# Router of the experts: low halves of x on another engine, exponentials ahead of a copy, a quarter of a product behind the ranks

## The reference, cut to what matters

```
h = rmsnorm(x, norm_ffn_g)
g_prob = softmax(h @ w_rg + b_rg);  g_top, g_idx = top_k(g_prob, 1)
e_in   = (h @ w_re + b_re)[group g_idx]
e_top, e_idx = top_k(softmax(e_in), 2)
wts = g_top * e_top / sum(e_top)
x = x + sum over the token's two experts e: wts * ((silu(h @ w_g[e]) * (h @ w_u[e])) @ w_d[e])
x = x + (p @ w_ple) * sigmoid(rmsnorm(x, norm_ple_g) @ w_ple_gate)
return rmsnorm(x, final_norm_g)
```

## Time and profile before

| | us |
|---|---|
| median of 3 runs | 1081.22 (1079.3 to 1083.87) |
| profiled execution | 1086.42 |
| its span (first to last instruction) | 1084.6 |
| TensorE busy | 1036.2 |
| VectorE busy | 627.4 |
| ScalarE busy | 534.5 |
| GpSimd busy | 89.8 |

### The profile page before, as it was taken

How to read it: one execution, slowest core, us unless ns; L and a number is a source line. 1 busy time by engine, 2 the same in 40 slices (tenths; PEclk the granted TensorE clock), 3 DMA queues, 4 the chain that set the end, 5 groups by cost and what they waited for, 6 DMA issues and landing times.

```text
span 1084.6 us, 15375 instructions
## 1 busy us (share of the span) xinstructions
PE 1036.2 (96%) x6023; PEld 795.3 (73%) x6023; DVE 627.4 (58%) x1235; ACT 534.5 (49%) x940; POOL 89.8 (8%) x104
## 2 busy tenths in 40 slices
PE   6998999999999999899999999998989999999987
PEld 5776589999988877599999889676754454545445
DVE  4677567888745566568888647757752121212155
ACT  5766465565535465556555435856532221212254
POOL 0101001122100311001212101100000000000000
PEclk8998699999999999999999999999999999999989
DMA  8824135655554533255664564224739999999921
GB/s 280 297 79 154 40 118 178 197 170 192 197 194 155 195 118 120 73 170 180 183 200 162 196 181 135 97 90 142 280 112 410 409 409 408 409 409 409 403 93 39
DMA packets 112672, 224.62 MB, mean 207 GB/s; under 512 B 10559, under 2 KB 65234, under 8 KB 112594
## 3 DMA queue, kind: packets, MB, share of 16 engines
q1 hardware_dynamic: 112434, 223.04, 58.7%
q10 hardware_dynamic: 160, 0.53, 0.1%
HBM read 222.50 MB, written 1.05 MB: 206 GB/s over the span
## 4 chain that ended last, share of the span: by engine, by line
PE 87%; DVE 6%; ACT 4%; issue 1%; DMA 1%; SPq 0%; DVEq 0%; ACTq 0%
PE ps L542 82%; PE ps L546 4%; DVE wl L1862 1%; ACT pb L1332 1%; DMA ring<-in_w_uv_dram 1%; DVE smb L1876 1%; ACT wh L1335 1%; ACT hh L1332 1%; DMA cst<-in_const_dram 0%; DVE hl L1872 0%; ACT L1332 0%; DVE ml L1862 0%; DVE pb L1867 0%; ACT mh L1335 0%; DVE sA L1872 0%
## 5 line engine op out<-in xcount | busy, mean ns | idle before, releaser
L1862 DVE TENSOR_TENSOR wl<-ring,wh 128x1024 fp32r<-128x1024 f32 (+3 forms) x212 | 278.1, 1321 | 128.4 <-ACT wh L1335 127.2
L1335 ACT ACTIVATE wh<-ring 128x1024 fp32r<-128x1024 f32 (+3 forms) x212 | 222.7, 1053 | 145.5 <-PE ps L542 145.0
L542 PE MATMUL ps<-hh,wh 128*128 128x256 f32 x768 | 219.0, 286 | 0.4 <-DVE big L1880 0.3
L542 PE MATMUL ps<-hh,wl 128*128 128x256 f32 x768 | 217.2, 284 | 0.0
L542 PE MATMUL ps<-hl,wh 128*128 128x256 f32 x768 | 215.4, 284 | 0.0
L542 PEld LDWEIGHTS ps<-hh,wh 128*128 128x128 f32 x768 | 147.7, 192 | 1.8 <-issue 1.4
L542 PEld LDWEIGHTS ps<-hh,wl 128*128 128x128 f32 x768 | 147.8, 192 | 0.0
L542 PEld LDWEIGHTS ps<-hl,wh 128*128 128x128 f32 x768 | 146.8, 192 | 0.2
L542 PE MATMUL ps<-ring,xg 128*64 128x512 f32 x320 | 85.5, 595 | 0.0
L542 PE MATMUL ps<-wh,hh 128*128 128x512 f32 (+3 forms) x192 | 80.2, 418 | 4.4 <-DVE wl L1862 4.3
L2702 POOL TENSOR_TENSOR fs<-fs,rt 128x256 f32<-128x256 f32 x44 | 52.4, 1213 | 322.8 <-ACT fs L1332 322.8
(11 more groups left out here) (284 smaller groups left out, 1715.7 us busy)
## 6 DMA issues: line engine op xcount, KB each, us to landing
ring<-in_w_up_dram SPq DMA_DIRECT2D x88, 512.0 KB, 4.7
ring<-in_w_down_dram SPq DMA_DIRECT2D x22, 1024.0 KB, 4.9
ring<-in_w_gate_e_dram SPq DMA_DIRECT2D x40, 512.0 KB, 7.9
ring<-in_w_up_e_dram SPq DMA_DIRECT2D x40, 512.0 KB, 9.3
ringx<-in_w_down_e_dram SPq DMA_DIRECT2D x16, 1024.0 KB, 8.6
ring<-in_w_down_e_dram SPq DMA_DIRECT2D x16, 1024.0 KB, 9.9
ring<-in_w_in_odd_dram SPq DMA_DIRECT2D x12, 1024.0 KB, 5.1
ringx<-in_w_gate_e_dram SPq DMA_DIRECT2D x24, 512.0 KB, 9.9
```

Source lines behind the costliest of these rows:

```text
L542: return e.matmul(o, l, r, start=start, stop=stop)
L1335: return e.activation(o, i, ACT.Copy)
L1862: return e.tensor_tensor(o, a, b, op)
```

## The change

Three edits.

1. The low halves move from VectorE to GpSimd, one behind the other, each behind its high half.
2. On ScalarE the exponentials of the logits come ahead of the high half of tile 1.
3. On TensorE the last quarter of the embeddings' product, (1, 1), comes behind the ranks; with it moves the point at which its weights' slot is free.

```diff
@@ tensor
-            for t in range(2):
-                for n in range(2):
-                    b = claim(2 * t + n, "ple", t, n)
-                    for k in range(2):
-                        w = mm(b[:, :], ppT[:, k, t * P:(t + 1) * P], up[:, k, n * 512:(n + 1) * 512], k == 0, k == 1)
-                    w.then_inc(of(full, "ple", t, n), 1)
-            unit_done[u_ple] = (of(full, "ple", 1, 1), use["ple", 1, 1][1] + 1)
+
+            def embedding(t, n):
+                b = claim(2 * t + n, "ple", t, n)
+                for k in range(2):
+                    w = mm(b[:, :], ppT[:, k, t * P:(t + 1) * P], up[:, k, n * 512:(n + 1) * 512], k == 0, k == 1)
+                w.then_inc(of(full, "ple", t, n), 1)
+
+            for t, n in ((0, 0), (0, 1), (1, 0)):
+                embedding(t, n)
             q.wait_ge(s_msk, 1)
             b = take("rank")
...
+            embedding(1, 1)
+            unit_done[u_ple] = (of(full, "ple", 1, 1), use["ple", 1, 1][1] + 1)
@@ scalar
-            copy(xhk[:, 1], xk[:, 1]).then_inc(s_xhi, 1)
             q.wait_ge(s_smi, 1)
             act(scr[:, 0:80], scr[:, 0:80], ACT.Exp).then_inc(s_sme, 1)
+            copy(xhk[:, 1], xk[:, 1]).then_inc(s_xhi, 1)
@@ vector
-            def x_lo(t):
-                q.wait_ge(s_xhi, t + 1)
-                tt(xlk[:, t], xk[:, t], xhk[:, t].bitcast(F32), ALU.subtract).then_inc(s_xlo, 1)
...
-            x_lo(0)
             b = filled(q, "route")
...
-            x_lo(1)
             b = filled(q, "rank")
@@ gpsimd
+            for t in range(2):
+                q.wait_ge(s_xhi, t + 1)
+                e.tensor_tensor(xlk[:, t], xk[:, t], xhk[:, t].bitcast(F32), ALU.subtract).then_inc(s_xlo, 1)
```

## The result

The changed kernel is slower: 1088.01 us median of 21 runs against 1083.38 of 21 of the kernel before, ratio 1.0044 with a 95% interval of [1.0031, 1.0058], some 4.7 us.

What follows compares the result with a forecast made beforehand. TensorE, busy for 96% of the span, was taken to bound the kernel. Order -1.72, VectorE's loss behind the ranks +0.3 and clock -1.35 sum to -2.8 us: 1078.4 against 1081.22, range 1075.3 to 1083.0.

Steps and rivals of the forecast that it cites:

- The place: Router up to the first expert's product: an earlier first product moves the rest of the kernel one for one.
- The quarter behind the ranks: TensorE ahead of the ranks: ranks start 1.72 us earlier with all edits, only 0.9 us without the other two.
- The clock gain of 1.35 us: Gather on TensorE: no clock fall after the ranks, so 3.85 us instead of 5.19.
- The gain of the logits taken early: VectorE's chain to the mask: logits taken at 782.5 instead of 784.22, 1.7 us earlier.
- Rival D: Experts behind the gather: DMA at 1.03 could hold them back and swallow the gain; 1081 us, chance 0.06.
- What GpSimd costs VectorE: VectorE's small operations beside GpSimd: slowed by 0.7 us up to the mask, 0.3 us lost behind the ranks.
- The upper end that I gave, 5.5 us: VectorE between exponentials and mask: at most 0.25 us lost on each of 22 small operations, ranks at 794.9.
- rival B: VectorE's small operations lose over 0.85 us, 0.1 each putting the mask at 791.6; 1079.8 to 1080.8 us, chance 0.12.
- right behind the third quarter: Ranks on TensorE: forecast to start at 790.24, when three quarters of the embeddings' product are done.
- if it had no cover: Last quarter between ranks and gather: hidden in idle time with 0.2 us to spare, otherwise costing its 1.72 us back.
- GpSimd's own duration: Each low half on GpSimd: 5.3 us taken, from 3.05 x 1.74, between ends of 3.05 and 8.6 us.
- Rival C: Low halves on GpSimd late for the gather, up to 8.6 us each, gather 3.9 us later; 1085.1 us, chance 0.12.

Runs made afterwards that it cites:

- e3: Kernel before with only the last quarter of the embeddings' product moved behind the ranks; ratio 0.9980 to the kernel before.
- e1: Changed kernel with both low halves back on VectorE at their old places, the other two edits kept; ratio 0.9990 to the kernel before.
- e4: Changed kernel with GpSimd computing one feature of 128 per tile, the gather reading high halves in place of low; ratio 0.9965 to the kernel before.
- e5: Changed kernel with each low half cut into eight GpSimd operations of 128 features; ratio 1.0006 to the kernel before.
- e6: Changed kernel with each low half computed twice on GpSimd, the second behind the first; ratio 1.0089 to the kernel before.
- e2: Kernel before with only the low halves moved to GpSimd, old order on ScalarE and TensorE; ratio 1.0039 to the kernel before.

## Why the prediction was wrong

**What held.** The place: experts follow the router one for one (30.73 us for two steps in both), and the stretch's 4.06 us are close to the 4.7 of the medians. The quarter behind the ranks gains by itself: in e3 the ranks start 0.77 us earlier, "only 0.9 us" in the prediction. The clock gain of 1.35 us, where TensorE does not stand idle ahead of the ranks for long: from the gather's start to the first expert's product it was 6.51 us at a granted clock of 0.78 before and 5.23 at 1.00 in e1, e3 and e4, 1.28 less. Here is e3's:

```profile
791.75:796.98 5.23, 5.23 (x45) 5.21 (x45) 4.44 (x17) 1.79 (x5) 0.00 (x0) 1.00 0.61 201
```

The gain of the logits taken early: in e4 all of it arrives, a mask 1.92 us earlier where 1.7 was forecast. Rival D, that the experts' DMA swallows everything, fell.

**The step that failed** is "What GpSimd costs VectorE", 0.7 us up to the mask and 0.3 behind it. In the sum the 0.7 counted for nothing, since a mask at 790.1 was still ahead of the third quarter at 790.24. Measured were two rows 5.19 us too long up to the mask (a mask about 4.5 us late, by the estimate under e4) and nothing behind it. I read two rows, two VectorE operations in 3.45 us beside two of GpSimd in 2.48, as both engines slowing by a share of the columns that they stream. By that a 64-column operation could lose 0.03 us. What e5 and e6 show is that the instruction waits for the rest of GpSimd's operation, whatever its own width. The same rows, with each instruction as a row of its own, show it in the trace of before:

```profile
559.81 0.79 POOL L2702 TENSOR_TENSOR fs<-fs,rt 128x256 f32<-128x256 f32 x1 [9.04 <-ACT fs L1332]
559.91 1.77 DVE L1862 TENSOR_TENSOR wl<-ring,wh 128x1024 fp32r<-128x1024 f32 x1
560.56 1.72 POOL L2702 TENSOR_TENSOR fs<-fs,rt 128x256 f32<-128x256 f32 x1
561.61 1.76 DVE L1862 TENSOR_TENSOR wl<-ring,wh 128x1024 fp32r<-128x1024 f32 x1
```

They end at 560.60, 561.68, 562.28 and 563.37: each engine's operation ends somewhat less than its own length behind the end of the other's, about 1.08 us for VectorE's (1.226 alone) and 0.60 for GpSimd's (0.72 alone). So they took turns, and GpSimd waited too: the 1.24 us that I read as its length beside VectorE stand for one operation of 0.79 us and one of 1.72. A loss of 0.54 us is as large as GpSimd's operations there allowed, and here they are 2.85 us long. The row of 398.74 was the hint: a 128x2 operation has nothing to stream, and lost 0.26 us all the same. It ends at 399.17, and the GpSimd operation beside it (398.68, 0.46 us) at 399.14. The upper end that I gave, 5.5 us, was about right, but it was made up of 22 small losses and not of two large ones, and I gave it no chance; rival B, which named the mechanism's place, was priced at 0.1 us for each operation. A second, smaller part of the miss is the base: the kernel before has its median at 1083.38, 2.2 us above the three runs that I had. And the lower end of the range, 1075.3, does not follow from its terms: 1078.4 - 0.3 - 2.5 is 1075.6.

**What followed from it.** TensorE idled 4.03 us where the ranks were forecast "right behind the third quarter". Behind the wait the ranks took 2.34 us, about twice their 1.20, and the quarter that should hide in the idle time ran at the lower clock too. The selection was written at 797.86, the gather started at 798.63; before, 0.15 us lay between the two (794.97 and 795.12). So the quarter, moved ahead of the gather, cost some 0.6 us more. Ranks to gather took 4.93 us, against 3.27 in e4, and gather to experts 6.34 at 0.87 against 5.23: 1.66 + 1.11 = 2.77, the rest of the 7.92. The prediction had the quarter cost 1.72 us "if it had no cover". The cover, the wait for the selection, was there; at the lower clock the quarter outlasted it.

**GpSimd's own duration** was missed the other way: 5.3 us taken, 2.85 and 2.88 measured. The 3.05 of the earlier trace rows that I started from holds a wait itself: a two-input operation of VectorE beside it ended at 662.22, and GpSimd's some 2.3 us later. Alone, the same width takes 2.44 us:

```profile
751.87 2.44 POOL L2726 TENSOR_TENSOR sA<-sA 128x1024 f32<-128x1024 f32 x1 [54.60 <-ACT sA L1332]
```

Against that row the steps of 128 elements (in one input and in the output) cost GpSimd about 0.4 us, a sixth; that VectorE pays 1.74 times for them was no guide. The Trainium skill, GPSIMD Engine Reference, section 7, gives half as much again for reads whose steps exceed 8 bytes. That is not seen here: 2.85 against 2.44 us. Rival C, low halves late for the gather, therefore never arose: they were done at 790.22, long before 798.63.

**A rule I should have weighed.** In the changed kernel's trace a copy within SBUF waits out GpSimd's operation. The Trainium skill has a rule of this kind in Advanced Engine Details and Errata, section VectorE Performance Modes: the second VectorE port is shared with GpSimd, and GpSimd's instructions and VectorE's two-port ones block each other. The traces agree on the blocking, and show it for two-input TENSOR_TENSORs too (0.24 to 2.72 us in e2), which that sentence does not name. I had cited only the softer word, contention, of another page, and put a share on it.

## What to carry to other kernels

A long GpSimd operation on SBUF is not free work beside VectorE: price it as the rest of its own length for the next VectorE instruction that moves data within SBUF or has two SBUF inputs, once for each GpSimd operation, however small that instruction is. Beside a chain of small dependent operations this is the worst place for it; if it must be there, cut it into short pieces (8 in place of 1 took 5.8 us out of the stretch and some 4 us out of the time here, which still left the kernel no faster than before). And work moved into an engine's wait is free only while it is shorter than that wait, at the clock that it will get: here the quarter was not.

## What the runs showed of the hardware

- Held beside GpSimd: a copy from SBUF to SBUF (0.19 us alone, 2.73 held), TENSOR_TENSOR with two SBUF inputs (0.24 alone, 2.72 held), and in e5 a TENSOR_SCALAR of 8 columns (0.17 and 0.45) and a SCALAR_TENSOR_TENSOR with all inputs in SBUF (0.23 and 0.42). Not held: TENSOR_REDUCE (0.24), SCALAR_TENSOR_TENSOR with one input in PSUM (0.42 for two, at 785.06 in e6), and in e5 a RECIPROCAL (0.22).
- A held instruction gets in between two GpSimd operations (e5, e6). GpSimd waits for VectorE's two-input operations in the same way: 1.72 us for one of 0.72 at 560.56 before. How the turn is decided no run here took apart.
- GpSimd's subtraction over 128x1024, with one input and the output stepping by 128 elements, takes 2.85 to 2.89 us (a contiguous product of this size 2.44), a copy with such an output 1.94 to 2.00. Cut into eight it is 0.49 us a piece, VectorE's turns included.
- Sixty-four columns or eight, it makes no difference to the hold: it is set by what is left of GpSimd's operation.
